# Two edits to a two-layer hybrid transformer kernel: down-projection splits kept across the column halves, and the mixer projection copied out of PSUM tile by tile

## The reference

```python
for layer in range(DEPTH):
    need_ctx = layer < DEPTH - 1
    y_l, y_c = mixer(modulate(x, sh1, sc1), modulate(ctx, csh1, csc1), w_in[layer], ...)
    x = post_norm(x, g1 * y_l, ln1_w[layer], ln1_b[layer])
    x = post_norm(x, g2 * swiglu(modulate(x, sh2, sc2), w_gate_up[layer], w_down[layer]), ...)
    ...                                   # the same for ctx where need_ctx

def swiglu(h, w_gu, w_dn):                # inner width 2816
    g, u = jnp.split(h @ w_gu, 2, axis=-1)
    return (jax.nn.silu(g) * u) @ w_dn
```

## Time and profile before

| what | value |
|---|---|
| median of 3 runs | 1706.0 us (1705.37 to 1706.23) |
| the profiled execution's own time | 1705.96 us |
| its span, first to last instruction | 1704.2 us |
| PE busy | 1628.7 us (96%) |
| DVE, ACT, POOL busy | 819.5, 448.8, 860.1 us |
| mean granted clock of TensorE | 0.991 |

### The profile page before, as it was taken

One profiled execution on the slowest core, in us unless ns is written; L12 is line 12 of the kernel. 1 busy time (PEld: TensorE's weight loads), 2 busy tenths in 40 slices (PEclk: granted clock), 3 DMA queues, 4 the chain that ended last, 5 costly groups with the idle time before them and its releaser, 6 DMA issues. The chain is left out here.

```text
span 1704.2 us, 23677 instructions
## 1 busy us (share of the span) xinstructions
PE 1628.7 (96%) x9500; PEld 1386.0 (81%) x9500; DVE 819.5 (48%) x1240; ACT 448.8 (26%) x937; POOL 860.1 (50%) x844
## 2 busy tenths in 40 slices
PE   6999999999899999999999999999999999999997
PEld 4777866768899997899998778786778988788885
DVE  5354254447673415444454684635557421520058
ACT  5511365433500011100002164125534200210021
POOL 4444034543464444544445571532576577677772
PEclk9999999999999999999999999999999999999999
DMA  9211033322343212243642120210023452233321
GB/s 363 77 50 54 22 108 119 104 80 62 100 142 118 91 64 68 65 146 113 209 161 77 57 86 25 74 50 8 14 64 97 141 149 93 93 99 99 99 87 50
DMA packets 157004, 160.93 MB, mean 94 GB/s; under 512 B 6376, under 2 KB 111960, under 8 KB 156896
## 3 DMA queue, kind: packets, MB, share of 16 engines
q1 hardware_dynamic: 136560, 121.40, 23.3%
q10 hardware_dynamic: 20336, 38.03, 6.8%
HBM read 157.31 MB, written 2.10 MB: 94 GB/s over the span
## 5 line engine op out<-in xcount | busy, mean ns | idle before, releaser
L682 POOL TENSOR_SCALAR ring_hi<-stage 128x512 fp32r<-128x512 f32 x352 | 248.4, 706 | 595.8 <-PE ps L758 569.3
L685 POOL TENSOR_TENSOR ring_lo<-stage,ring_hi 128x512 fp32r<-128x512 f32 x352 | 491.4, 1396 | 29.4
L756 PE MATMUL ps<-act_hi,ring_hi 128*128 128x384 f32 (+2 forms) x1088 | 379.6, 349 | 0.0
L758 PE MATMUL ps<-act_hi,ring_lo 128*128 128x384 f32 (+2 forms) x1088 | 378.0, 347 | 0.0
L757 PE MATMUL ps<-act_lo,ring_hi 128*128 128x384 f32 (+2 forms) x1088 | 377.9, 347 | 0.0
L756 PE MATMUL ps<-ring_hi,act_hi 128*128 128x512 f32 (+1 forms) x700 | 280.4, 401 | 11.2 <-DVE act_lo L1863 5.0
L758 PE MATMUL ps<-ring_hi,act_lo 128*128 128x512 f32 (+1 forms) x700 | 272.4, 389 | 0.0
L757 PE MATMUL ps<-ring_lo,act_hi 128*128 128x512 f32 (+1 forms) x700 | 272.3, 389 | 0.0
L758 PEld LDWEIGHTS ps<-act_hi,ring_lo 128*128 128x128 f32 x1088 | 204.6, 188 | 13.3
L757 PEld LDWEIGHTS ps<-act_lo,ring_hi 128*128 128x128 f32 x1088 | 204.7, 188 | 12.9
L756 PEld LDWEIGHTS ps<-act_hi,ring_hi 128*128 128x128 f32 x1088 | 204.6, 188 | 12.9
(11 more groups left out here) (267 smaller groups left out, 2147.8 us busy)
## 6 DMA issues: line engine op xcount, KB each, us to landing
stage<-in_w_gate_up_dram SPq DMA_DIRECT2D x88, 512.0 KB, 5.0
mod_stage<-in_w_mod_dram ACTq DMA_DIRECT2D x56, 512.0 KB, 4.3
stage<-in_w_in_dram SPq DMA_DIRECT2D x18, 1024.0 KB, 5.1
stage<-in_w_down_dram SPq DMA_DIRECT2D x16, 1024.0 KB, 5.0
stage<-in_w_mod_dram SPq DMA_DIRECT2D x12, 1024.0 KB, 5.3
start_mod<-in_w_mod_dram SPq DMA_DIRECT2D x8, 1024.0 KB, 11.2
stage<-in_w_down_dram SPq DMA_DIRECT2D x8, 768.0 KB, 4.4
stage<-in_w_out_dram SPq DMA_DIRECT2D x16, 256.0 KB, 4.5
```

The lines of the kernel that those rows point to most:

```text
L682: nc.gpsimd.tensor_scalar(hi_, stage[:, par, j * 512:(j + 1) * 512], 1.0, 0.0, ALU.mult, ALU.add).then_inc(w_hi, 1)
L685: nc.gpsimd.tensor_tensor(lo_, stage[:, par, j * 512:(j + 1) * 512], hi_.bitcast(F32), ALU.subtract).then_inc(w_ready, 1)
L756: nc.tensor.matmul(o, a_hi, b_hi, start=first, stop=False)
L758: return nc.tensor.matmul(o, a_lo, b_hi, start=False, stop=last)
```

## The change

It has two parts. **Down:** `KEPT` = (3, 8) names how many split chunks stay in their slots from the first to the second pass of a half. The second pass starts with those chunks (`hid_chunk`) and only splits the other 8 (half 0) or 3 (half 1), 11 + 8 + 11 + 3 = 33 splits a layer. The weight rows of `w_down` are loaded in that order. DVE makes all residuals of the first pass directly behind its low parts. **Projection:** the copy of a tile out of PSUM waits for that tile of the block before alone and only ahead of the copy to `pre`; and the transposes of the last tile (layer 0) or the last two (layer 1) of blocks 0 and 1 go behind slice 0 (and 1) two blocks later. In layer 1 the first transpose of blocks 0 and 1 goes behind slice 3, not 2.

```diff
-            "gu0": [4] * HALF, "dn0": [4, 4, 3] * 2, "gu1": [4] * HALF, "dn1": [4, 4, 3] * 2}
+            "gu0": [4] * HALF, "dn0": [4, 4, 3, 3, 4, 4], "gu1": [4] * HALF, "dn1": [4, 4, 3, 4, 4, 3]}
+KEPT = (3, 8)
...
+        def held_back(l, b):
+            return 0 if b == 2 else 1 + l
...
+        def hid_chunk(p, q):
+            return (q + p % 2 * (HALF - KEPT[p // 2])) % HALF
+        def splits_to(p, q):
+            kept = KEPT[p // 2]
+            before = p // 2 * (2 * HALF - KEPT[0])
+            return before + q + 1 if p % 2 == 0 else before + HALF + max(q + 1 - kept, 0)
+        def hid_slot(p, q):
+            kept = KEPT[p // 2]
+            s = (q + p % 2 * (HALF - kept)) % kept
+            return (hs_hi[:, s, :], hs_lo[:, s, :]) if p < 2 else (act_hi[:, s, :], act_lo[:, s, :])
+        def hid_slot_wait(e, l, p, q):
+            if q >= KEPT[p // 2]:
+                e.wait_ge(ring_used, dn_slot(l, p, q - KEPT[p // 2]) + 1)
...
@@ SP, the order of the rows of w_down
-                        k0 = f0 + 4 * (i % 3)
+                        q = sum(SEGMENTS[seg][3 * (i // 3):i])
+                        k0 = f0 + hid_chunk(2 * int(seg[2]) + i // 3, q)
...
@@ PE, project
-                        late = 1 if b == 3 else 2
-                        if b > 0 and late <= j < late + len(block_tiles(l, b - 1)):
+                        if b >= 2 and j == 0:
+                            tpose(b - 2, NT - held_back(l, b - 2), ALL[NT - held_back(l, b - 2)])
+                        if b >= 2 and j == (0 if b == 3 else 1) and held_back(l, b - 2) == 2:
+                            tpose(b - 2, NT - 1, ALL[NT - 1])
+                        late = 1 if b == 3 else 2 + l
+                        if b > 0 and late <= j < late + len(block_tiles(l, b - 1)) - held_back(l, b - 1):
                             tpose(b - 1, j - late, block_tiles(l, b - 1)[j - late])
...
@@ ACT, project
-                        for n, t in enumerate(block_tiles(l, b - 1)):
-                            read_T(b - 1, n, t)
+                        if b >= 2:
+                            for n in range(NT - held_back(l, b - 2), NT):
+                                read_T(b - 2, n, ALL[n])
+                        pb = block_tiles(l, b - 1)
+                        for n in range(len(pb) - held_back(l, b - 1)):
+                            read_T(b - 1, n, pb[n])
...
-                        if 0 < b < 4:
-                            need(act, "post_ready", l, pre_count(l, b - 1, len(block_tiles(l, b - 1)) - 1))
                         acc = ps[:, t, :]
                         if b < 2:
                             a.activation(v_attn["AB"[b]][:, t, :], acc[:, 384:512], ACT.Copy)
+                        if b > 0:
+                            pb = b - 1 if t in block_tiles(l, b - 1) else b - 2
+                            need(act, "post_ready", l, pre_count(l, pb, block_tiles(l, pb).index(t)))
+                        if b < 2:
                             w = slice(256 if kv_only(l, b, t) else 0, 384)
                             ins = a.activation(pre[:, t, w], acc[:, w], ACT.Copy)
...
@@ DVE, hid_lows and down_low
-                p, by_tile = 2 * fh, 3 if fh else 2
+                p = 2 * fh
                 hid_lows(l, p, range(4 if fh else 1, HALF))
-                hid_lows(l, p + 1, range(by_tile))
                 for n, t in enumerate(tiles):
                     residual(l, "dn", p, n, t, nt, dn_slot(l, p, HALF - 1), 0, fh == 0)
                     if fh == 1:
                         link(half_stats(t, 0, 0))
-                    if n == nt - 2:
-                        hid_lows(l, p + 1, [by_tile])
-                hid_lows(l, p + 1, range(by_tile + 1, HALF))
+                hid_lows(l, p + 1, range(KEPT[fh], HALF))
```

More of the change, by code:

```diff
@@ L391, in part_place @@
             return ps[:, r + f * len(tiles_of(l)) // 2, gu * 256:gu * 256 + 256], slice(c0, c0 + 256)
[L393 to L406, removed]
+        def hid_chunk(p, q):
[11 more added lines that the diff above has]
+                e.wait_ge(ring_used, dn_slot(l, p, q - KEPT[p // 2]) + 1)
             elif p >= 2:
-                e.wait_ge(ring_used, SLOT0[(l, "gu1")] + 4 * (HALF - 1) + n // 2 + 1)
+                e.wait_ge(ring_used, SLOT0[(l, "gu1")] + 4 * (HALF - 1) + q // 2 + 1)
         def attn_pairs(l):
@@ L550, in signals @@
                 "gn_var": 2, "gn_sd_ready": 2, "y_ready": 2, "y_hi": 2, "y_lo": 2, "norm_in": 64, "silu_ready": 2 * HALF, "hid_ready": 2 * HALF,
-                "hid_hi": 4 * HALF, "hid_split": 4 * HALF, "wout_read": 2 * nt, "dn_read": 4 * nt,
+                "hid_hi": splits_to(3, HALF - 1), "hid_split": splits_to(3, HALF - 1), "wout_read": 2 * nt, "dn_read": 4 * nt,
             }[name]
@@ L731, in _ @@
                     if n < 0:
-                        need(pool, "hid_split", l - 1, 4 * HALF)
+                        need(pool, "hid_split", l - 1, splits_to(3, HALF - 1))
                         for j in range(-n):
@@ L1330, in arrived @@
                     pe.wait_ge(w_ready, seg_slot[p] + j + 1)
-                    need(pe, "hid_split", l, p * HALF + j + 1)
+                    need(pe, "hid_split", l, splits_to(p, j))
                 for dh in range(2):
@@ L1371, in down @@
                                   lambda j, s: tuple(h[:, s] for h in hid_slot(3, 3 + j)),
-                                  lambda j: need(pe, "hid_split", l, 3 * HALF + 3 + j + 1))
+                                  lambda j: need(pe, "hid_split", l, splits_to(3, 3 + j)))
             pe.wait_ge(sem("start_set"), 1)
@@ L1696, in load_norm, with hid_high @@
                 act.dma_start(bc[:, 3, :], b[l].partition_broadcast(P)).then_inc(sem("norm_in"), 16)
-            def hid_high(l, p, j):
+            def hid_high(l, p, q):
                 cols = slice(0 if l < DEPTH - 1 else CTX, TOK)
+                j = hid_chunk(p, q)
                 need(act, "hid_ready", l, p // 2 * HALF + j + 1)
-                hid_slot_wait(act, l, p, j)
-                a.activation(hid_slot(p, j)[0][:, cols], hid[:, j, cols], ACT.Copy).then_inc(sem("hid_hi"), 1)
+                hid_slot_wait(act, l, p, q)
+                a.activation(hid_slot(p, q)[0][:, cols], hid[:, j, cols], ACT.Copy).then_inc(sem("hid_hi"), 1)
             def gate_half(l, fh):
@@ L1747, in down_hi @@
                 for p in (2 * fh, 2 * fh + 1):
-                    for j in range((4 if fh else 2) if p % 2 == 0 else 0, HALF):
+                    for j in range((4 if fh else 2) if p % 2 == 0 else KEPT[fh], HALF):
                         if p == 0 and j == 3:
@@ L2228, in retention, with hid_lows @@
                 scaled_low(1)
-            def hid_lows(l, p, js):
+            def hid_lows(l, p, qs):
                 cols = slice(0 if l < DEPTH - 1 else CTX, TOK)
[L2233 to L2236, removed]
+                for q in qs:
+                    hi_, lo_ = hid_slot(p, q)
+                    need(dve, "hid_hi", l, splits_to(p, q))
+                    done(low(lo_[:, cols], hid[:, hid_chunk(p, q), cols], hi_[:, cols]), "hid_split")
             def up_half(l, fh):
```

## The result

| | time, us | ratio to before, 95% interval |
|---|---|---|
| before | 1705.68 median (1704.56 to 1706.39, 6 runs) | |
| after | 1695.65 median (1693.72 to 1697.95, 6 runs) | 0.9946 [0.9935, 0.9956] |
| predicted | 1694.5 (1689.5 to 1699.5) | |

The change takes 10.0 us off. The profiled execution of after took 1693.95 (span 1691.8).

A forecast was written before the change was run, and what follows sets the result against it. PE was taken as busy nearly throughout at full clock, so time is won only where it waits. 2.8 - 0.6 + 1.65 + 2.7 + 2.5 + 2.4 = 11.45 off 1705.96 gives 1694.5 us, range 1689.5 to 1699.5.

The forecast's parts named there:

- A: Projection, layer 0: PE's waits at two block boundaries go; 2.8 us won.
- B: Projection, layer 1: DVE's later chain makes PE idle over 4 us for tile 5, then half clock; 0.6 us lost.
- C: Pass 0 to pass 1, layer 0: PE's waits on residuals go; 1.65 us won.
- D: Pass 3, layer 0: fewer low parts, POOL's splits late next; 2.7 us won, ends 0.9 and 4.4.
- F: Pass 3, layer 1: POOL's three splits less stretched and started earlier; 2.4 us won, ends 1.5 and 3.3.
- E: Pass 0 to pass 1, layer 1: PE's waits on residuals go; 2.5 us won.
- POOL did take DVE's place in pass 3: Rival, pass 3: POOL replaces DVE as what is late, D 0.9 and F 1.5; 1697.2 us, 17%.
- No stall in layer 1: Rival, layer 1's projection: DVE stretched less, half clock stays away, B 3 to 5.8 won; 1688 to 1691 us, 15%.
- Slower: Rival, layer 1's `post`: eight latent arrangements on PE's path, decisive from 1.9 us more on each; 1712.1 at 2.2, 3%.

The follow-up runs named there:

- bytile_only: The changed kernel with no transposes held back (`late` = 2) and the copies to `pre` by tile kept; 1698.58 us, one execution.
- short_lows: The changed kernel with the low parts of pass 3 cut to 16 columns, leaving out the rest; 1692.12 us, ratio 0.992.
- order_only: The kernel before, with DVE's first residual of pass 0 ahead of the low parts of pass 1; 1705.18 us against 1705.19, ratio 0.9997.
- l1_late2: The changed kernel with layer 1's first transpose of blocks 0 and 1 behind slice 2 again, not slice 3; 1691.53 us, ratio 0.9929.
- held_only: The changed kernel with copies to `pre` waiting for the last tile of the block before again, transposes still held back; 1702.62 us, one execution.
- before_late1: The kernel before, with layer 1's transposes of blocks 0 and 1 behind slices 1 to 4 instead of 2 to 5; 1701.04 us, ratio 0.9977.

## Why the prediction was right, point by point

The total was right within 1.2 us, by terms that mostly held. The sum of the ledger, with N set aside, is 2.91 - 1.48 + 2.09 + 2.58 + 2.63 + 2.01 = 10.7 against 11.45; with the longer last write, which I had not foreseen, it is 9.8. That the profiled execution took 1693.95, even nearer to 1694.5, is luck: it is 12.0 under before's, of which 3.8 are an earlier start.

- **A, 2.8 predicted, 2.91 measured.** Both waits went. But I gave the copies by tile half the credit; bytile_only shows that they had none.
- **B, 0.6 lost predicted, 1.48 lost.** The mechanism held. I put the end of tile 5's copy 34.85 behind the start of block 1; it was 1078.32 + 0.49 - 1044.04 = 34.77. PE's idle time was 3.25 + 0.32 = 3.57, where I had 1089.0 - 1084.7 = 4.3. ACT's copy in after:

```profile
1078.32 0.49 ACT L1532 ACTIVATE pre<-ps 128x384 f32<-128x384 f32 x1 [3.56 <-DVE post L2006]
```

and PE's start behind it:

```profile
1078.86 0.80 PE L768 MATMUL ps<-ring_hi,act_hi 128*128 128x512 f32 x1 [3.25 <-ACT pre L1532]
```

  The term that was mis-sized is the half clock. I charged 3.4 us of it, 1.7 lost, as behind the idle time of 1.90 before. Behind the longer one it was twice as long (columns as above):

```profile
1077.20:1084.10 6.90, 5.24 (x14) 4.17 (x15) 1.28 (x4) 0.98 (x2) 1.89 (x2) 0.51 0.37 141
```

  From 1078.86 to 1084.07 PE worked at the lower of its two levels, 1.2 GHz: about 2.6 lost instead of 1.7, which is the miss. The wait in block 3 came as well, 0.20 for 0.4.
- **C, 1.65 predicted, 2.09.** The waits went. I counted two of them; between them four more tiles had started 0.07 late each without showing a wait, 0.3 in all. The other 0.15 is not placed.
- **D, 2.7 predicted, 2.58; F, 2.4 predicted, 2.01.** POOL is what is late next, as forecast. PE of after in pass 3, layer 0 and layer 1:

```profile
966.20 0.50 PE L768 MATMUL ps<-ring_hi,act_hi 128*128 128x512 f32 x1 [1.69 <-POOL ring_lo L697]
...
1663.85 0.50 PE L768 MATMUL ps<-ring_hi,act_hi 128*128 128x512 f32 x1 [0.96 <-POOL ring_lo L697]
```

  A low part stretched POOL's three splits by 0.66 in layer 0 (0.5 taken) and by 0.41 in layer 1 (7.18 - 5.94, over three; 0.27 taken). Dividing the stretch of before by seven low parts was too kind: three splits are six instructions of POOL, and in before each of them was stretched once (by 0.40 to 0.70 in layer 0, by 0.14 to 0.44 in layer 1), so that seven low parts shared the price of six; in after three of the six are stretched. The far ends, 4.4 and 3.3, are near what short_lows gives, 4.54 and 3.24; they leave out the 0.25 and 0.15 between POOL's end and PE's start that the middle values have, and would be 4.2 and 3.2 with them. By the rule cited from the Trainium skill ("SBUF — State Buffer", "Who interferes with whom"), each low part would hold POOL for its own 0.96; the trace shows two thirds of that.
- **E, 2.5 predicted, 2.63.** Held.
- **The rivals.** POOL did take DVE's place in pass 3, but at a smaller price than the rival's. "No stall in layer 1" is refuted, and its reason too: DVE is stretched more, not less, when PE does not wait. "Slower" needed 1.9 us more on each arrangement; the chain of four was 19.9 as before.

## What to carry to other kernels

Where one engine works through a chain that another engine's step sets off, write down when it starts, how long it is and when its last product is wanted; moving the step by a slice is one digit of the code and won 2.95 by itself, twice what the reordering around it brought (1.7 of it, by estimate, as the clock stayed up). Before an order is changed to take a wait away, add up what the engine has to do in the stretch: order_only moved two low parts and won 0.3, since the sum did not fit. And compare executions by lengths between fixed instructions: they agreed within 0.05 us where whole times differed by 3, but look at the granted clock in each length (N moved by 1.3), and see what lies behind the last length.

## What the runs showed of the hardware that I had not expected

DVE and POOL hold each other up in both directions. Three low parts of 768 columns cost POOL 1.98, and took DVE 5.18 beside POOL, where one takes 0.96 beside nothing. Cut to 16 columns the three still took 1.94. DVE of short_lows:

```profile
960.17 1.94 DVE L1885 TENSOR_TENSOR act_lo<-hid,act_hi 128x16 fp32r<-128x16 f32 x3 [1.80 <-ACT act_hi L1726]
```

The three took 1.15, 0.54 and 0.17: the first two ended at 961.33 and 961.90, within 0.04 of the end of an instruction of POOL (961.29 and 961.88), the third started in the 0.09 between two of them. So what a small instruction of DVE costs beside POOL's splits is the rest of the instruction that POOL is at, not its own size.

A stretch at half clock lasted 3.4 or 6.8 us within the layers. In layer 1's projection it was 3.4 with an idle time of 1.90 (before) or 1.81 (l1_late2) and 6.8 with 3.25 (after) or 6.64 (held_only). The length of the idle time alone does not decide it: before_late1 idled 2.30 in block 1, and held_only 2.20 in block 3, and the granted clock stayed at 1.00 behind both. Where such a stretch falls on a PE that waits anyway it costs nothing, where it falls on work it costs half its length; that moved N by 1.3 us. The start moved by up to 3.8 between executions; how much of that is the clock was not worked out.

The last write of the output has 512 KB. In the eight profiles in which it took 3.6, one packet of 8 KB of the queue for instructions moved during it; in the five in which it took 2.6, none did. From the view of DMA of after, 1687 to 1692:

```profile
q14 instruction: 1, 0.01, 0.4%
```

That the packet is what holds the write up is likely by this but not tested; no run moved it by itself.
